# Where the inverse is applied in a chunked delta rule: to the decayed keys ahead of the scan, or to beta v minus keys times state inside it

## The chip, the cores and the metric

The kernel runs on one core of one Trainium2 chip. The metric is the device time of one execution in microseconds (us), the median of several runs. The engines are named as in the profile: PE is the matrix engine (PEld its weight loads), DVE the vector engine, ACT the scalar engine, POOL the engine that here makes small sums and DMA issues, SP the queue that issues the weight loads.

## The reference

Two transformer-like blocks on 512 tokens of width 1024. The first block has a gated delta-rule layer (8 heads, keys of 128, values of 256) and a windowed attention layer; the second has four feed-forward layers, a pooling layer and a convolution module. The change is in the delta rule alone:

```python
def step(S, inp):                      # one chunk; every head has a state S of (128, 256)
    qk_i, qd_i, kd_i, u_i, w_i, gl_i = inp
    v_new = u_i - w_i @ S
    o = qd_i @ S + qk_i @ v_new
    S = S * gl_i + kd_i.T @ v_new
    return S, o
# ahead of the loop, for each chunk:
#   decay = exp(g[:, None] - g[None, :]) below the diagonal, g a running sum of log decays
#   lower = strict_lower(beta * (k @ k.T) * decay)
#   u, w  = solve(I + lower, [beta * v, beta * exp(g) * k])
#   qk = (q @ k.T) * decay;  qd = q * exp(g);  kd = k * exp(g_last - g);  gl = exp(g_last)
```

The kernel takes chunks of 128 tokens, so there are 4 chunks where the reference has 8 of 64; the result is the same sum.

## The kernel before, in words

**Order of stages.** Each engine has its own list of instructions, written out by hand, and semaphores tie them together. The delta-rule layer comes first and ends at about 557 us. It works through 4 pairs of heads (`pe_a`, `act_a`, `dve_a`, `gp_a`, called with i = 0 to 3). The `Marks` objects `a_pe`, `a_act`, `a_dve` and `a_gp` count the named steps of each engine, and `wait` waits for a step by its name.

**Filler.** The weights come in tiles of 128x2048. ACT rounds a tile (L354), DVE subtracts the rounded part from the raw one (`split_tile`, L359), and PE multiplies with both parts, three matmuls for one product. While PE works on a pair of heads it also makes the projections for the gate of this pair and for the queries, keys and values of the next one: six tiles of 16 steps, 96 steps in all, each of three matmuls (L768 to L770). `pe_filler` hands them out: `fill(n)` issues the next n steps, and `fill()` all that are left. A pair before the last one spends its 96 steps as 55 ahead of the scan over the chunks (up to the `fill(2)` of L897), 16 in the scan (two behind the `vn` products of each chunk and two behind the `sn` products), 6 behind the scan (L929), and the last 19 behind the column sums `os` (L939). The last pair has only 32 steps, since there is no next pair, and they run out with chunk 0 of the scan. Behind the filler of a pair stand its two output tiles (L941, which calls `pe_tile`: 16 chunks of 6 matmuls, L382 to L384).

**The scan.** For each chunk c and each of the two heads a, PE makes `vn`: `inv_T` times `v_beta` (L909) and, from chunk 1 on, `neg_wT` times `state` into the same accumulator (L911). ACT copies it to `v_new` (L1052). PE makes the outputs `o` (L921, L922) and the update of the state `sn` (L926). DVE writes the new `state` (L1239 in chunk 0, L1242 after it). `neg_wT` is made ahead of the scan: DVE multiplies the turned keys with beta and decay (`k_bg`, L1179), PE multiplies that with `inv_T` (`nw`, L901), and ACT copies it with the sign turned (L1046). In float32 each product is two instructions of the trace.

**DVE beside the scan.** Its list is: `convolved(0)` (two L1114, six L1117) for the next pair, the two states of chunk 0, `split(4)`, the states of chunks 1 and 2, `convolved(2)`, `split(5)`, the four gated outputs `og` (L1253), and, once the norm of the output is there, `gt` (L1261), `split(6)`, the pair of rounded outputs (L1093), `convolved(4)`, and only then `add_chunks` (L427), which adds the output tile to `xT` chunk by chunk. A chunk n of the output tiles may start on PE only when DVE has added chunk n - 4 (the wait on `out_free` in `pe_tile`), since there are four PSUM banks for them. The norm itself runs from `os` on PE over two logarithms (L1067) and two exponentials (L1070) on ACT, then `take(5)` (L955), a rounding (L354) and the rounded outputs (L1076).

## Time and profile before

| | |
|---|---|
| median of 3 runs | 2715.42 us (2711.14 to 2717.76) |
| the profiled execution | 2712.42 us |
| its span, first to last instruction | 2710.8 us |
| mean granted PE clock | 0.983 |
| busy share PE, PEld, DVE, ACT, POOL | 97%, 78%, 57%, 37%, 13% |
| DMA | 238 MB, mean 88 GB/s |

A time in the trace counts from the start of the span. Busy shares are over the whole span; a matmul's busy time includes its way through the array, so the distance from start to start of successive matmuls is what one costs in a row of them. The first pair of heads occupies PE from about 87 to 213 us, the second to 340 us, the third to 467 us, and the last one to about 557 us.

### The profile page before, as it was taken

The page shows a single profiled execution, that of the slowest core. Times are in us where ns is not written, and L with a number is a line of the kernel's source. Part 1 is how long each engine was busy: PE and PEld are TensorE (multiplying, and loading weights), DVE is VectorE, ACT ScalarE, POOL GpSimd, SP SyncE. Part 2 cuts the span into 40 slices and gives each one's busy share as a digit, 9 for nine tenths or more (in the row PEclk, how much of TensorE's full clock was granted, in tenths as well). Part 3 has the DMA queues.
Part 4 walks back from the last instruction along what each step waited for, and adds up shares of the span by engine and source line. Part 5 has one row for each costly group of instructions (what it writes and reads, how often), then busy time and mean ns, then how long its engine had stood idle before and what let it go on. Part 6 is the DMA issues. An engine that isn't in the chain of part 4 may idle for free.

```text
span 2710.8 us, 37439 instructions
## 1 busy us (share of the span) xinstructions
PE 2631.8 (97%) x14593; PEld 2112.3 (78%) x14593; DVE 1547.4 (57%) x2261; ACT 1001.1 (37%) x1414; POOL 360.9 (13%) x330
## 2 busy tenths in 40 slices
PE   7999999899999979999999999999999897999998
PEld 5787878687777758888888888888888664888887
DVE  6666756576666664454555444654444776644445
ACT  4544444446556542222252222332222313422223
POOL 1110101022000011111131111121112120211110
PEclk8999999999999979999989999999999998999999
DMA  3222223122222212222312322222322452222321
GB/s 114 82 84 72 78 64 98 43 71 78 78 85 77 75 50 94 93 93 96 105 47 93 102 99 93 93 94 98 103 93 94 119 157 56 94 93 94 106 94 62
DMA packets 171509, 238.23 MB, mean 88 GB/s; under 512 B 6513, under 2 KB 149371, under 8 KB 171411
## 3 DMA queue, kind: packets, MB, share of 16 engines
q1 hardware_dynamic: 163523, 217.23, 24.2%
q0 software_dynamic: 6080, 19.43, 2.6%
q8 instruction: 69, 1.13, 0.2%
q10 hardware_dynamic: 1808, 0.21, 0.1%
q14 instruction: 29, 0.24, 0.0%
HBM read 232.36 MB, written 4.40 MB: 87 GB/s over the span
## 4 chain that ended last, share of the span: by engine, by line
PE 88%; DVE 5%; DMA 2%; ACT 2%; issue 2%; POOL 1%; DVEq 0%; SPq 0%; ACTq 0%; POOLq 0%
PE ps L382 20%; PE ps L383 20%; PE ps L384 20%; PE ps L768 5%; PE ps L770 4%; PE ps L769 4%; PE ps L368 1%; DVE w_lo L359 1%; PE ps L370 1%; PE ps L369 1%; DMA glu_scratch<-glu 1%; DVE probs L1633 1%; PE ps L1491 1%; PE ps L1502 1%; DMA shifted<-glu_scratch 1%
## 5 line engine op out<-in xcount | busy, mean ns | idle before, releaser
L354 ACT ACTIVATE w_hi<-w_raw 128x2048 fp32r<-128x2048 f32 x203 | 388.5, 1914 | 911.6 <-PE ps L384 901.5
L382 PE MATMUL ps<-h_hi,w_hi 128*128 128x512 f32 x1456 | 567.7, 390 | 0.0
L384 PE MATMUL ps<-h_hi,w_lo 128*128 128x512 f32 x1456 | 566.6, 389 | 0.0
L383 PE MATMUL ps<-h_lo,w_hi 128*128 128x512 f32 x1456 | 566.4, 389 | 0.0
L359 DVE TENSOR_TENSOR w_lo<-w_raw,w_hi 128x2048 fp32r<-128x2048 f32 x203 | 464.8, 2290 | 129.5 <-ACT w_hi L354 129.4
L427 DVE SCALAR_TENSOR_TENSOR xT<-ps,xT 128x512 f32<-128x512 f32 x504 | 336.5, 688 | 146.8 <-PE ps L384 145.7
L382 PE MATMUL ps<-a_hi,w_hi 128*128 128x512 f32 x1024 | 401.8, 392 | 17.1 <-issue 17.1
L383 PE MATMUL ps<-a_lo,w_hi 128*128 128x512 f32 x1024 | 401.1, 392 | 0.0
L384 PE MATMUL ps<-a_hi,w_lo 128*128 128x512 f32 x1024 | 400.9, 392 | 0.0
L1718 POOL TENSOR_TENSOR f_gate<-f_gate,n_rstd 128x512 f32<-128x512 f32 x88 | 176.9, 2012 | 1121.8 <-ACT f_gate L1712 1121.8
L382 PEld LDWEIGHTS ps<-h_hi,w_hi 128*128 128x128 f32 x1456 | 273.3, 188 | 59.3 <-issue 2.5
L384 PEld LDWEIGHTS ps<-h_hi,w_lo 128*128 128x128 f32 x1456 | 273.3, 188 | 56.7
L383 PEld LDWEIGHTS ps<-h_lo,w_hi 128*128 128x128 f32 x1456 | 273.3, 188 | 56.6
L768 PE MATMUL ps<-h_hi,w_hi 128*128 128x512 f32 x608 | 260.2, 428 | 1.4 <-DVE w_lo L359 1.4
L382 PEld LDWEIGHTS ps<-a_hi,w_hi 128*128 128x128 f32 x1024 | 194.1, 190 | 60.1 <-issue 19.5
L770 PE MATMUL ps<-h_hi,w_lo 128*128 128x512 f32 x608 | 238.1, 392 | 0.0
L769 PE MATMUL ps<-h_lo,w_hi 128*128 128x512 f32 x608 | 237.3, 390 | 0.0
L383 PEld LDWEIGHTS ps<-a_lo,w_hi 128*128 128x128 f32 x1024 | 194.0, 190 | 40.4
L384 PEld LDWEIGHTS ps<-a_hi,w_lo 128*128 128x128 f32 x1024 | 193.8, 189 | 40.5
L1772 DVE TENSOR_TENSOR f_hid<-f_gate,ps 128x512 f32<-128x512 f32 x88 | 60.5, 688 | 252.6 <-PE ps L384 246.3
L1763 DVE TENSOR_TENSOR f_gate<-ps,n_rstd 128x512 f32<-128x512 f32 x88 | 60.5, 691 | 233.2 <-PE ps L384 233.1
L768 PEld LDWEIGHTS ps<-h_hi,w_hi 128*128 128x128 f32 x608 | 114.1, 188 | 40.2 <-issue 16.1
(337 smaller groups left out, 2820.9 us busy)
## 6 DMA issues: line engine op xcount, KB each, us to landing
w_raw<-in_ffn_w_in_dram SPq DMA_DIRECT2D x88, 1024.0 KB, 5.0
w_raw<-in_ffn_w_out_dram SPq DMA_DIRECT2D x44, 1024.0 KB, 4.8
w_raw<-in_a_w_in_dram SPq DMA_DIRECT2D x24, 1024.0 KB, 5.3
w_raw<-in_b_w_in_dram SPq DMA_DIRECT2D x16, 1024.0 KB, 5.4
w_raw<-in_conv_w_pw_dram SPq DMA_DIRECT2D x12, 1024.0 KB, 5.7
shifted<-glu_scratch POOLq DMA_DIRECT2D x32, 264.0 KB, 4.7
w_raw<-in_a_w_out_dram SPq DMA_DIRECT2D x8, 1024.0 KB, 4.8
w_raw<-in_b_w_out_dram SPq DMA_DIRECT2D x8, 1024.0 KB, 4.8
```

The costliest lines, as they stand in the source:

```text
L354: nc.scalar.activation(w_hi[:, t % 2], w_raw[:, t % 2], ACT.Copy).then_inc(hi_done, 1)
L359: nc.vector.tensor_tensor(w_lo[:, t % 2], w_raw[:, t % 2], w_hi[:, t % 2].bitcast(F32), ALU.subtract).then_inc(lo_done, 1)
L382: nc.tensor.matmul(dst, wh, xh, start=(k == 0), stop=False)
L383: nc.tensor.matmul(dst, wh, xl, start=False, stop=False)
L384: m = nc.tensor.matmul(dst, wl, xh, start=False, stop=last)
L427: ins = nc.vector.scalar_tensor_tensor(xT[:, n], src, scale, xT[:, n], ALU.mult, ALU.add)
L768: nc.tensor.matmul(dst, wh[:, w], h_hi[:, k], start=k == 0, stop=False)
L769: nc.tensor.matmul(dst, wh[:, w], h_lo[:, k], start=False, stop=False)
L770: ins = nc.tensor.matmul(dst, wl[:, w], h_hi[:, k], start=False, stop=k == KC - 1)
L1718: nc.gpsimd.tensor_tensor(f_gate[:, c], f_gate[:, c], n_rstd[:], ALU.mult).then_inc(f_gated, 1)
L1763: nc.vector.tensor_tensor(f_gate[:, c], ps[:, c], n_rstd[:], ALU.mult).then_inc(in_free, 1)
L1772: nc.vector.tensor_tensor(f_hid[:, c], f_gate[:, c], ps[:, 2 + c], ALU.mult).then_inc(in_free, 1)
```

## The change

The product of the inverse with the decayed keys is no longer made. Instead, in chunks 1 to 3, PE multiplies the keys with the state (`ks`), DVE scales the result with beta and decay and subtracts `v_beta` from it (`r`, written over `v_beta`), and PE multiplies the inverse with that (`vn`). The sign is turned in ACT's copy. `k_bg`, `nw` and `neg_wT` are gone. In the scan a `fill(2)` (`fill(1)` in the last pair) stands between `ks` and `vn`; DVE's two `r` of a chunk stand behind its two states, ahead of `split(4)` in chunk 0.

```diff
--- before.py
+++ after.py
@@ -232,7 +232,7 @@
             z_gate = sb("z_gate", [P, 4, T], into=s)
         rel_in, rel_T = z_gate[0:BUCKETS, 2, 0:B_HEADS], z_gate[0:B_HEADS, 2, P:P + BUCKETS]
         rel_line = z_gate[0:B_HEADS, 3, 0:3 * P]
-        inv_T, neg_wT, k_bg = g_wide, decay, expg
+        inv_T = g_wide
 
 
         binv_T, binv = b_wide[:, 0, 0:8 * BK], b_wide[:, 0, 8 * BK:16 * BK]
@@ -609,23 +609,23 @@
                      + [x for l in lv for x in [f"A{l}", f"X{l}"]
                         + ([f"vt{a}{l - 2}" for a in heads] if l in (2, 3) else [])]
                      + ["A5", "X5", "A6", "X6"]
-                     + [f"nw{a}" for a in heads]
-                     + [f"{x}{c}{a}" for c in range(TC) for x in (("vn", "o", "sn") if c < TC - 1 else ("vn", "o"))
+                     + [f"{x}{c}{a}" for c in range(TC)
+                        for x in [y for y in ("ks", "vn", "o", "sn") if not (y == "ks" and c == 0 or y == "sn" and c == TC - 1)]
                         for a in heads]
                      + [f"os{a}" for a in heads])
         a_act = Marks(sem("a_act"), [f"sq{c}" for c in (2, 3, 0, 1)] + [f"ln{c}" for c in (2, 3, 0, 1)]
                       + [f"rs{c}" for c in (2, 3, 0, 1)]
                       + [f"eg{a}" for a in heads] + [f"d{a}" for a in heads]
                       + ["blocks", "dg"]
-                      + [f"nw{a}" for a in heads] + [f"vn{c}{a}" for c in range(TC) for a in heads]
+                      + [f"vn{c}{a}" for c in range(TC) for a in heads]
                       + [f"os{a}{d}" for a in heads for d in range(2)] + [f"oln{a}" for a in heads]
                       + [f"ors{a}" for a in heads])
         a_dve = Marks(sem("a_dve"), [f"nrm{c}" for c in (2, 3, 0, 1)]
                       + [f"{x}{a}" for a in heads for x in ("db", "lt")] + ["u0", "u1", "T0", "qk0", "qd0"]
-                      + ["P1", "qk1", "qd1", "U1", "T1", "kb0", "kd0", "P2", "kb1", "kd1", "U2", "T2"]
+                      + ["P1", "qk1", "qd1", "U1", "T1", "kd0", "P2", "kd1", "U2", "T2"]
                       + ["P3", "vb00", "vb01", "U3", "T3", "P4", "vb10", "vb11", "U4", "T4"]
                       + ["P5", "U5", "P6", "U6"]
-                      + [f"S{c}{a}" for c in range(TC - 1) for a in heads]
+                      + [f"{x}{c}{a}" for c in range(TC - 1) for x in ("S", "r") for a in heads]
                       + [f"og{a}{d}" for a in heads for d in range(2)]
                       + [f"gt{a}{d}" for a in heads for d in range(2)])
         a_gp = Marks(sem("a_gp"), [f"msk{a}" for a in heads] + ["zero"] + [f"osum{a}" for a in heads])
@@ -895,26 +895,20 @@
                          inv_T[hi, a, c * P + 64:c * P + P], start=True, stop=True)
             a_pe.done("X6", ins)
             fill(2)
-            for a in heads:
-                a_dve.wait(pe, "U6", i)
-                for c in range(TC):
-                    ins = mm(pb(2 + a, c), v(k_bg, a, c), v(inv_T, a, c), start=True, stop=True)
-                a_pe.done(f"nw{a}", ins)
+            a_dve.wait(pe, "U6", i)
             for c in range(TC):
+                if c:
+                    for a in heads:
+                        a_dve.wait(pe, f"S{c - 1}{a}", i)
+                        a_pe.done(f"ks{c}{a}", mm(ps[:, 4 + a, 0:A_DV], v(qkv, 2 + a, c), state[:, a], start=True, stop=True))
+                    fill(2 if ahead > 1 else 1)
                 for a in heads:
-                    b = ps[:, 4 + a, 0:A_DV]
                     if c:
-                        a_dve.wait(pe, f"S{c - 1}{a}", i)
-                        a_act.wait(pe, f"nw{a}", i)
-                    ins = mm(b, v(inv_T, a, c), v_beta[:, a, c], start=True, stop=c == 0)
-                    if c:
-                        ins = mm(b, v(neg_wT, a, c), state[:, a], start=False, stop=True)
-                    a_pe.done(f"vn{c}{a}", ins)
-                fill(1 if last_pair(i) else 2)
+                        a_dve.wait(pe, f"r{c - 1}{a}", i)
+                    a_pe.done(f"vn{c}{a}", mm(ps[:, 4 + a, 0:A_DV], v(inv_T, a, c), v_beta[:, a, c], start=True, stop=True))
+                fill(2 if ahead > 1 else 1)
                 for a in heads:
                     a_act.wait(pe, f"vn{c}{a}", i)
-                    if c == 0:
-                        a_act.wait(pe, "nw1", i)
                     for d in range(2):
                         b = pb((2, 3, 6, 7)[2 * a + d], c)
                         if c:
@@ -1041,15 +1035,12 @@
             a_act.done("dg", ins)
             take(1)
             rounded(4)
-            for a in heads:
-                a_pe.wait(act, f"nw{a}", i)
-                a_act.done(f"nw{a}", fn(neg_wT[:, a], ps[:, 2 + a], ACT.Copy, scale=-1.0))
             for c in range(TC):
                 for a in heads:
                     a_pe.wait(act, f"vn{c}{a}", i)
                     if c:
                         a_pe.wait(act, f"sn{c - 1}{a}", i)
-                    a_act.done(f"vn{c}{a}", fn(v_new[:, a], ps[:, 4 + a, 0:A_DV], ACT.Copy))
+                    a_act.done(f"vn{c}{a}", fn(v_new[:, a], ps[:, 4 + a, 0:A_DV], ACT.Copy, scale=-1.0 if c else 1.0))
                 if c == 0:
                     take(2)
                 elif c == 2:
@@ -1176,7 +1167,6 @@
                 wide = lambda name, n: gate_col(name, i, a).to_broadcast([P, TC, n])
                 a_pe.wait(dve, f"kt{a}", i)
                 a_dve.wait(dve, f"qd{a}", i)
-                a_dve.done(f"kb{a}", v.tensor_tensor(by_chunk(k_bg[:, a]), by_chunk(ps[:, 2 + a]), wide("beta_exp", P), ALU.mult))
                 a_dve.done(f"kd{a}", v.tensor_tensor(by_chunk(k_dec[:, a]), by_chunk(ps[:, 2 + a]), wide("k_decay", P), ALU.mult))
 
             def values(d):
@@ -1241,6 +1231,11 @@
                         decayed = gate["last"][:, c, bass.ds(i * 2 + a, 1)]
                         ins = v.scalar_tensor_tensor(state[:, a], state[:, a], decayed, ps[:, 4 + a, A_DV:], ALU.mult, ALU.add)
                     a_dve.done(f"S{c}{a}", ins)
+                for a in heads:
+                    a_pe.wait(dve, f"ks{c + 1}{a}", i)
+                    a_dve.done(f"r{c}{a}", v.scalar_tensor_tensor(
+                        v_beta[:, a, c + 1], ps[:, 4 + a, 0:A_DV], gate["beta_exp"][:, c + 1, bass.ds(i * 2 + a, 1)],
+                        v_beta[:, a, c + 1], ALU.mult, ALU.subtract))
                 if c == 0:
                     split(4)
             convolved(2)
```

## Rows read from the trace of the kernel before

**Rows 1.** The page: engines' busy time, the chain that ended last, a weight load.
```profile
PE 2631.8 (97%) x14593; PEld 2112.3 (78%) x14593; DVE 1547.4 (57%) x2261; ACT 1001.1 (37%) x1414; POOL 360.9 (13%) x330
...
PE 88%; DVE 5%; DMA 2%; ACT 2%; issue 2%; POOL 1%; DVEq 0%; SPq 0%; ACTq 0%; POOLq 0%
...
w_raw<-in_a_w_in_dram SPq DMA_DIRECT2D x24, 1024.0 KB, 5.3
```

**Rows 2.** PE's waits, 80 to 560 us: total us, times, longest.
```profile
PE ps L382 <- issue: 6.5, 1, 6.5
PE ps L768 <- DVE w_lo L359: 1.4, 1, 1.4
PE ps L851 <- DVE b_wide L1199: 0.3, 1, 0.3
```

**Rows 3.** Timeline of PE, first pair, chunks 0 to 2: start us, us, instruction, count.
```profile
145.09 1.95 PE L901 MATMUL ps<-g_wide,expg 128*128 128x128 f32 x16
146.88 1.03 PE L909 MATMUL ps<-v_beta,g_wide 128*128 128x256 f32 x4
...
152.28 0.59 PE L909 MATMUL ps<-v_beta,g_wide 128*128 128x256 f32 x2
152.71 0.59 PE L911 MATMUL ps<-state,decay 128*128 128x256 f32 x2
...
159.44 0.59 PE L909 MATMUL ps<-v_beta,g_wide 128*128 128x256 f32 x2
```

**Rows 4.** Timeline of DVE and ACT, same stretch; in brackets idle before, and releaser.
```profile
145.09 4.05 DVE L1117 SCALAR_TENSOR_TENSOR qkv<-conv_in,cols,qkv 128x512 f32<-128x512 f32 x6
...
151.43 2.28 DVE L359 TENSOR_TENSOR w_lo<-w_raw,w_hi 128x2048 fp32r<-128x2048 f32 x1
...
165.80 0.88 DVE L1114 TENSOR_SCALAR qkv<-conv_in,cols 128x512 f32<-128x512 f32 x2
...
170.57 2.29 DVE L359 TENSOR_TENSOR w_lo<-w_raw,w_hi 128x2048 fp32r<-128x2048 f32 x1
...
153.34 0.38 ACT L1052 ACTIVATE v_new<-ps 128x256 f32<-128x256 f32 x1 [4.11 <-PE ps L911]
```

**Rows 5.** DVE's groups by shape, 80 to 560 us: count, busy us, mean ns.
```profile
L1242 DVE SCALAR_TENSOR_TENSOR state<-state,gate_last,ps 128x256 f32<-128x256 f32 x16 | 7.3, 480 | 39.1 <-PE ps L926 39.1
...
L1179 DVE TENSOR_TENSOR expg<-ps,gate_beta_exp 128x512 f32<-128x512 f32 x8 | 5.3, 666 | 0.0
```

**Rows 6.** Timeline of PE behind the scan, first pair.
```profile
176.97 1.88 PE L937 MATMUL ps<-square,ones 128*128 128x512 f32 x4
178.29 0.79 PE L768 MATMUL ps<-h_hi,w_hi 128*128 128x512 f32 x1
...
179.39 0.40 PE L768 MATMUL ps<-h_hi,w_hi 128*128 128x512 f32 x1
...
190.98 0.39 PE L768 MATMUL ps<-h_hi,w_hi 128*128 128x512 f32 x1
191.66 0.39 PE L382 MATMUL ps<-a_hi,w_hi 128*128 128x512 f32 x1
...
197.10 0.39 PE L382 MATMUL ps<-a_hi,w_hi 128*128 128x512 f32 x1
...
213.42 0.39 PE L768 MATMUL ps<-h_hi,w_hi 128*128 128x512 f32 x1
```

**Rows 7.** Timelines of ACT and DVE behind the scan, first pair.
```profile
181.95 0.58 ACT L955 ACTIVATE conv_in<-ps 128x512 f32<-128x512 f32 x1
...
189.78 4.06 DVE L1117 SCALAR_TENSOR_TENSOR qkv<-conv_in,cols,qkv 128x512 f32<-128x512 f32 x6
193.75 1.52 DVE L427 SCALAR_TENSOR_TENSOR xT<-ps,xT 128x512 f32<-128x512 f32 x2
195.94 0.69 DVE L427 SCALAR_TENSOR_TENSOR xT<-ps,xT 128x512 f32<-128x512 f32 x1 [0.67 <-PE ps L384]
197.30 0.69 DVE L427 SCALAR_TENSOR_TENSOR xT<-ps,xT 128x512 f32<-128x512 f32 x1 [0.67 <-PE ps L384]
...
211.86 2.48 DVE L427 SCALAR_TENSOR_TENSOR xT<-ps,xT 128x512 f32<-128x512 f32 x4
```

**Rows 8.** Timeline of the last pair's scan.
```profile
515.17 0.86 DVE L1239 COPY state<-ps 128x256 f32<-128x256 f32 x2 [5.57 <-PE ps L926]
...
516.09 0.59 PE L909 MATMUL ps<-v_beta,g_wide 128*128 128x256 f32 x2
...
520.78 0.70 PE L909 MATMUL ps<-v_beta,g_wide 128*128 128x256 f32 x2
...
521.31 0.59 PE L911 MATMUL ps<-state,decay 128*128 128x256 f32 x2
...
522.61 0.38 PE L921 MATMUL ps<-qn,state 128*128 128x128 f32 x2
...
528.96 0.39 PE L922 MATMUL ps<-qk_T,v_new 128*128 128x128 f32 x2
```

**Rows 9.** Windows: length; busy us of PE, PEld, DVE, ACT, POOL; granted clock; DMA.
```profile
521.00:526.00 5.00, 4.86 (x30) 4.17 (x30) 1.12 (x4) 3.17 (x4) 0.00 (x0) 1.00 0.00 0
...
534.00:540.00 6.00, 0.17 (x1) 0.20 (x2) 3.98 (x7) 4.92 (x8) 0.00 (x0) 0.78 0.00 0
540.00:544.00 4.00, 4.00 (x10) 3.13 (x11) 1.62 (x3) 0.00 (x0) 0.00 (x0) 0.50 0.02 4
```

## The prediction

> **What bounds the kernel now.** I read the page first. PE is busy 97% of the span and carries 88% of the chain that ended last [rows 1]. Then I listed PE's waits in the stretch of the delta rule. In some 470 us it waits 6.5 us once (ahead of the last pair's output tiles), 1.4 us once, and a few tenths besides [rows 2]. So the three pairs with full filler, from 87 to 467 us, are PE back to back, and there only two things count: PE work that goes, and a wait that appears. The last pair has no filler in chunks 1 to 3 and shows its own chain. Last I read the timelines of the scan and of what follows it, to see how far the other engines run ahead of PE. The reader should look at the places where PE and DVE nearly meet. In the first pair DVE adds the first chunk of the output tile at 193.75 to 194.44 (0.69 us, the duration of one L427) [rows 7], and PE, which may not start chunk 4 before that, starts it at 197.10 [rows 6]. The slack is 2.66 us. The three pairs repeat each other to 0.1 us.
>
> **What the change removes.** The `nw` products are 16 instructions of PE, from 145.09 to the next product at 146.88: 1.79 us a pair [rows 3], 7.2 us in four pairs. Two DVE operations of 0.67 us [rows 5] and two ACT copies a pair go as well. DVE and ACT wait for PE around there, in the full pairs and nearly so in the last, so I count these at nothing. The Trainium skill, page "TensorE: Matmul & The Clock Gate", section "Back-to-back issue gap", has about 81 ns for each matmul of 128 columns in a stream of loads and matmuls. By it the 64 instructions would be an estimated 5.2 us. The row has 1.79 / 16 = 0.112 us, and the sum goes by the row.
>
> **What it adds on PE: nothing in number.** From chunk 1 on `ks` takes the place of the `neg_wT` product and `vn` that of the `inv_T` product, both 128x256 in two instructions of 0.22 us (0.43 us from 152.28 to 152.71) [rows 3].
>
> **The new wait inside the scan, full pairs.** PE now needs DVE's `r` between `ks` and `vn`. A result of PE is read 0.63 us after its product starts (L911 at 152.71, the copy at 153.34) [rows 3, 4]. `r` is not in the trace; the nearest row is L1242, same form and size, one operand in PSUM: 0.48 us [rows 5]. Bounds are 0.4 and 0.7 us. So `r` of the first head ends 1.1 us behind the start of `ks`, that of the second 1.6 us. PE comes to `vn` after two `ks` (0.87 us) and two filler steps (1.36 us), at 2.2 us, and to the second head's at 2.7. The slack is 1.1 us for both, more than the upper bound takes. Cost nothing; without this cover 0.4 to 0.7 us in each of nine chunks.
>
> **What queues behind `r` on DVE.** In chunk 0 it is `split(4)`, which was made from 151.43 [rows 4]. It moves to about 152.1 to 154.4; its tile is wanted from step 65, about 158.3. In chunk 2 it is `convolved(2)` and `split(5)`. A chunk took 7.16 us (152.28 to 159.44) [rows 3] and takes 8.5 with two more filler steps. `convolved(2)`, from 165.80 before, waits for `r` of chunk 3 and starts at about 169.1, and `split(5)` ends at about 176.2 where it ended at 172.9 [rows 4]. Its tile is wanted at step 81, now at about 177.3. The slack of 1.1 us is thin, but it holds. SP's load of the tile two further on starts after each split and takes 5.3 us [rows 1]; `split(5)` releases that of the second output tile, whose rounding comes some 16 us later.
>
> **The filler that moves.** This is the part that costs. Three more blocks of two steps are spent in the scan of a full pair, and the total of 96 doesn't grow. So 13 steps instead of 19 are left behind `os`. Between 176.97 and 191.66 PE covered the norm, the gating and the rounding of the outputs [rows 6], which start with `os` and keep their length. A step is 0.68 us (18 from 179.39 to 191.66) [rows 6], so PE comes 6 x 0.68 = 4.1 us sooner to the output tile, counted from `os`. First it meets `take(5)` on ACT, which frees the bank for step 89: done 5.6 us behind `os` (182.53 - 176.97) [rows 7], wanted five steps behind `os`, at 2.42 + 4 x 0.68 = 5.1 (2.42 from 176.97 to 179.39, `os` and one step) [rows 6], a stall of 0.4. Then it meets the first `add_chunks`, behind `convolved(4)` in DVE's list, which ends 17.47 us behind `os` (194.44 - 176.97). PE wants chunk 4 at 20.13 - 4.08 = 16.05 us. The stall is 1.42 us in all, the first one included. From there DVE has no idle time to give back: its list up to the last addition fills 19.2 us (193.75 to 214.34 without the two idle times of 0.67) [rows 7], and PE's 12 chunks of 1.36 and the next pair's first 4 steps, behind which the additions must be done, fill 19.1. So each full pair gains 1.79 - 1.42 = 0.37 us, three gain 1.1. Bounds: 0 (DVE needs a further 0.4 us there) and 1.79 a pair (no stall).
>
> **The last pair.** It gains the 1.79 us of `nw`. Its filler ends in chunk 0 before and after, so `r` lies bare in chunks 1 to 3. Before, PE restarted 0.04 us behind `state` (520.78), and `o` followed 1.83 us behind that (522.61) [rows 8]. Now, counted from `ks`: `r` of the first head may start at 0.10 + 0.63 (a restart costs 0.10, as 520.78 to 521.31 is 0.53 where 0.43 is usual) and ends at 1.2. `vn` runs from 1.25, its result can be read at 1.25 + 0.10 + 0.63 = 2.0, and ACT's copy of 0.38 us [rows 4] ends at 2.4. `o` starts at about 2.45 or, with another restart, as at 2.5: 0.65 us later than before, in three chunks 1.95 us. Bounds by `r` of 0.4 and 0.7 us: 1.7 and 2.6. The pair nets +0.2 (-0.1 to +0.8).
>
> **The sum.** -3 x 0.37 + 0.2 = -0.9 us. The profiled execution took 2712.4 us (span 2710.8), so 2711.5 on its own scale. The median of the three runs is 3.0 us above it; the same change from there gives 2714.5 us. That is 0.03%. What a measurement of this kernel can tell from no change is about 0.3%, 8.1 us.
>
> **Rivals.**
> - *The whole of `nw` is won.* DVE's tail isn't met, since the filler steps or DVE's list run otherwise than I add them up. Full pairs give -5.4, the last +0.2: 2710.2 us; with the last pair's `r` free too, 2708.3. For it: PE is the bound by the page. Against it: the slack of 2.66 us is smaller than the 4.1 us that move. Chance 0.12. It too stays within 0.3%.
> - *DVE's list breaks the cover further.* `r` or `split(5)` comes late, or chunks 10 to 15 of the outputs wait for DVE. With 1 us more in each full pair it is 2717.5 us, with 2 us 2720.5. Against it are the slacks above. Chance 0.14.
> - *The other side: PE's clock falls in the last pair's scan.* In 534 to 540 us PE is busy 0.17 of 6 us, the granted clock there averages 0.78, and it is 0.50 in the next 4 us, the lower of its two levels, 1.2 GHz [rows 9]. In 521 to 526, with PE busy 4.86 of 5 us, it stayed at 1.00. The change adds two or three short waits a chunk to the 0.5 us there. If that made it fall, the 13 us from 516.09 to 528.96 [rows 8] would nearly double: +12 us, 2726 us, slower by 0.4%. It decides if the granted clock of these windows is below about 0.7 throughout. The page named above, section "HAM oscillation", warns of just this, a half clock from idle time between bursts of matmuls; whether such short gaps do it no row here shows. Chance 0.04.
> - *The change is not neutral before the scan.* Something that I count as covered, such as the missing `k_bg` on DVE in the last pair's short filler, speeds up its chain by the 2.7 us of four operations at most: 2711.8 us. Chance 0.05.
>
> **Numbers.** My forecast has 0.65, and the cases above follow. Likeliest 2714.5 us. The range goes from 2708.3 (all won) to 2720.5 (2 us more of DVE in each pair), 2708 to 2721; outside it lie the clock's case and a part of what the medians scatter. Faster by over 0.3% (below 2707.3) would need more than the 7.2 us that go away: 0.03. Slower (above 2723.6) is the clock's case and a rest of the second: 0.06. Within: 0.91.
>
> **What would show it.** In the trace after, `nw` is gone and DVE's `r` is an operation of 0.48 us, 24 times (three chunks, two heads, four pairs); PE waits for it only in the last pair, about 0.3 us each time. In each full pair PE waits about 0.4 us at a filler step (for ACT, L955) and 1 us at chunk 4 of the first output tile (for DVE, `add_chunks`). The distance from pair to pair is 126.6 us instead of 126.9. A pair distance of 125.1 shows the first rival right, one of 127 or more the second. The granted clock of the last scan shows the third.

## The result and the profile after

In nine runs of each kernel on one chip, the kernel before had a median of 2717.76 us (2711.14 to 2719.65) and the changed kernel 2723.78 us (2714.09 to 2731.73). The ratio on record is 1.0028, with an interval of 1.0015 to 1.0040; it is not the quotient of the two medians, which is 1.0022. By the medians the change is slower by 6.0 us, a little under what I had said such a measurement can tell; with nine runs the interval leaves 1 out. The profiled execution took 2730.16 us, with a span of 2727.6 us against 2710.8 before. The forecast was 2714.5 us, 2708 to 2721, so the result lies outside its range.

The page of the changed kernel, its first line of busy time and its chain, the counterpart of [rows 1]:

```profile
PE 2641.4 (97%) x14529; PEld 2114.4 (78%) x14529; DVE 1551.7 (57%) x2277; ACT 996.8 (37%) x1406; POOL 361.1 (13%) x330
...
PE 86%; DVE 6%; ACT 2%; DMA 2%; issue 2%; POOL 1%; DVEq 0%; ACTq 0%; POOLq 0%
```

PE has 64 instructions fewer, the `nw` products, and yet its busy time is 9.6 us longer. Part of this work must have been done at a lower clock: the mean granted clock is 0.978 where it was 0.983. The waits of PE from 80 to 575 us (in total, times, longest) say where to look; beside them, [rows 2] has three:

```profile
PE ps L382 <- issue: 6.5, 1, 6.5
PE ps L382 <- DVE xT L427: 2.2, 3, 0.7
PE ps L858 <- issue: 2.0, 1, 2.0
PE ps L768 <- DVE w_lo L359: 1.4, 1, 1.4
PE ps L768 <- ACT conv_in L949: 0.8, 3, 0.3
```

Two of the new lines come three times, once in each pair with full filler, and are the stalls of the forecast. The third comes once and was in no part of the forecast: 2.0 us at L858, the small products of the inverse (step `X4`), and nothing that the profile shows released PE from it. It lies in the last pair. PE's timeline there:

```profile
498.61 0.39 PE L770 MATMUL ps<-h_hi,w_lo 128*128 128x512 f32 x1
498.93 0.43 PE L858 MATMUL ps<-b_wide 32*32 32x32 f32 x26
501.41 0.63 PE L858 MATMUL ps<-b_wide 32*32 32x32 f32 x38 [2.05 <-issue]
501.97 0.80 PE L768 MATMUL ps<-h_hi,w_hi 128*128 128x512 f32 x1
```

The 64 products of one burst are cut after the 26th. No wait stands in the program between them, and in the kernel before they took 0.75 us in one piece. What follows the hole is the greater loss. Windows of the changed kernel (columns as in [rows 9]; the last three are granted clock, DMA share, GB/s):

```profile
497.00:498.00 1.00, 1.00 (x66) 0.64 (x64) 0.00 (x0) 0.00 (x0) 0.00 (x0) 1.00 1.09 387
498.00:499.00 1.00, 1.00 (x22) 0.56 (x14) 0.85 (x2) 0.00 (x0) 0.00 (x0) 1.00 0.90 313
499.00:500.00 1.00, 0.36 (x26) 0.25 (x26) 0.77 (x2) 0.00 (x0) 0.00 (x0) 1.00 0.03 9
500.00:501.00 1.00, 0.00 (x0) 0.00 (x0) 0.00 (x0) 0.00 (x0) 0.00 (x0) 1.00 0.05 6
501.00:502.00 1.00, 0.59 (x39) 0.53 (x39) 0.00 (x0) 0.00 (x0) 0.00 (x0) 0.81 0.00 0
502.00:504.00 2.00, 2.00 (x23) 1.25 (x21) 0.87 (x2) 0.34 (x1) 0.00 (x0) 0.50 0.03 8
...
516.00:518.00 2.00, 2.00 (x6) 1.60 (x5) 0.14 (x1) 0.00 (x0) 0.00 (x0) 0.50 0.00 0
518.00:520.00 2.00, 2.00 (x9) 1.61 (x8) 0.00 (x0) 0.77 (x2) 0.00 (x0) 0.83 0.00 0
```

The same windows of the kernel before:

```profile
498.00:499.00 1.00, 1.00 (x66) 0.64 (x64) 0.00 (x0) 0.00 (x0) 0.00 (x0) 1.00 1.08 383
499.00:500.00 1.00, 1.00 (x22) 0.58 (x17) 0.87 (x2) 0.00 (x0) 0.00 (x0) 1.00 0.86 301
500.00:501.00 1.00, 1.00 (x66) 0.91 (x67) 1.00 (x3) 0.00 (x0) 0.00 (x0) 1.00 0.09 28
```

PE does nothing in 500 to 501, and from 502 to 518 the granted clock is 0.50, the lower level of 1.2 GHz, though PE is busy all the time. Before, it stayed at 1.00. The hole and the half clock together are the loss of the last pair: from the start of the last pair (L816, at 468.96 after and 469.99 before) to its first output tile it is 79.34 us where it was 69.84. The tile in the timelines, first after, then before:

```profile
548.30 0.76 PE L382 MATMUL ps<-a_hi,w_hi 128*128 128x512 f32 x1 [6.50 <-issue]
```

```profile
539.83 0.77 PE L382 MATMUL ps<-a_hi,w_hi 128*128 128x512 f32 x1 [6.50 <-issue]
```

That is 9.5 us more. Of the 16.8 us by which the two profiled spans differ, most of the rest are 4.9 us in the pooling stage, which has a second stretch at half clock at 1399 to 1413 us, and 3.5 us in the convolution stage. Both come back to below.

**What arrived late.** In both kernels the 1 MB load of `w_kv`, the weights of the attention stage, comes over the DMA engines at this time: in the windows above it fills them up to 499 after, and up to 500 before. The trace also has the transfers that bring PE's instructions, in blocks of 16 KB on a queue of their own (q8, 68 blocks in the run). From 493 us on the changed kernel has no such block until 499.0. The kernel before has one at 495.3, just ahead of the load's first packets (496.5). In straight parts of the program one block comes for every 256 or so instructions of PE: from the one at 482.0 to the one at 531.7 us it is 1545 instructions for six blocks. While PE goes round a loop, as from 713 to 926 us, none comes.

By 499.0 PE had started 438 instructions since the block before; elsewhere in the last pair it was 116 to 302, and before 176 to 353. The change takes 40 PE instructions out of each pair (160 in all, 30233 to 30073, those that the profile doesn't count as busy included), so the borders of the blocks fall at other places of the program.

### The profile page after: what moved, and what is told of

It is laid out like the page before. It is cut to its first block, busy times and chain, and to the rows that moved or that the text cites. A ratio compares the mean times of both kernels' runs of the same rounds, so it can differ in the third digit from the quotient of the medians.

```text
span 2727.6 us, 37287 instructions
## 1 busy us (share of the span) xinstructions
PE 2641.4 (97%) x14529; PEld 2114.4 (78%) x14529; DVE 1551.7 (57%) x2277; ACT 996.8 (37%) x1406; POOL 361.1 (13%) x330
## 3 DMA queue, kind: packets, MB, share of 16 engines
q8 instruction: 68, 1.11, 0.2%
## 4 chain that ended last, share of the span: by engine, by line
PE 86%; DVE 6%; ACT 2%; DMA 2%; issue 2%; POOL 1%; DVEq 0%; ACTq 0%; POOLq 0%
PE ps L382 20%; PE ps L384 20%; PE ps L383 20%; PE ps L768 4%; PE ps L770 4%; PE ps L769 4%; DVE w_lo L359 1%; DMA glu_scratch<-glu 1%; PE ps L368 1%; PE ps L370 1%; PE ps L369 1%; DVE probs L1628 1%; PE ps L1486 1%; PE ps L1497 1%; DMA shifted<-glu_scratch 1%
## 5 line engine op out<-in xcount | busy, mean ns | idle before, releaser
L382 PE MATMUL ps<-a_hi,w_hi 128*128 128x512 f32 x1024 | 402.3, 393 | 19.2 <-issue 17.1
L427 DVE SCALAR_TENSOR_TENSOR xT<-ps,xT 128x512 f32<-128x512 f32 x504 | 335.5, 687 | 142.1 <-PE ps L384 141.6
```

What stands on the lines that cost most here:

```text
L382: nc.tensor.matmul(dst, wh, xh, start=(k == 0), stop=False)
L427: ins = nc.vector.scalar_tensor_tensor(xT[:, n], src, scale, xT[:, n], ALU.mult, ALU.add)
```

## The experiments

**Theory S (supply).** PE ran out of instructions: the block that it needed at `X4` of the last pair was fetched late, because the load of `w_kv` held the DMA engines. The hole then let the clock fall. The change causes it only through the place of a block's border. **Rival T (tail).** The loss is the change's own: DVE's list and the bare `r`, as in the rivals of the forecast. **Rival N (noise).** The half clock comes and goes by itself and the first nine runs fell unluckily.

The texts below that were written ahead of the runs call S theory F. Their theory C is a part of T: the bare waits of the last scan lower the clock.

Medians in us; ratio to the kernel before, measured beside it on the same chip (its medians were 2717.8 for the first nine runs, 2717.0 beside after_again, the pads of 136 and 120 and after_late_load, 2718.3 beside after_again2, before_gap2 and after_balanced, and 2717.2 beside the rest), with its interval; stage: from the end of PE's first long wait behind 80 us, where the work for the first pair begins, to the last pair's first output tile, in the one profiled execution.

| run | median (range), runs | ratio [interval] | stage |
|---|---|---|---|
| before, first profile | 2717.8 (2711.1 to 2719.7), 9 | 1 | 453.5 |
| after, first profile | 2723.8 (2714.1 to 2731.7), 9 | 1.0028 [1.0015, 1.0040] | 462.8 |
| after_again | 2721.3 (2717.5 to 2732.2), 12 | 1.0021 [1.0009, 1.0033] | 454.5 |
| after_again2 | 2724.8 (2716.4 to 2728.8), 12 | 1.0022 [1.0012, 1.0031] | 457.9 |
| after_late_load | 2719.2 (2711.1 to 2725.8), 12 | 1.0003 [0.9991, 1.0016] | 453.0 |
| before_late_load | 2716.6 (2711.4 to 2719.7), 11 | 0.9998 [0.9989, 1.0007] | 452.9 |
| before_pad136 | 2733.2 (2726.3 to 2735.5), 5 | 1.0063 [1.0050, 1.0076] | 454.2 |
| after_pad120 | 2723.4 (2716.6 to 2734.2), 8 | 1.0035 [1.0021, 1.0050] | 453.5 |
| after_pad60 | 2722.2 (2713.8 to 2726.0), 11 | 1.0013 [1.0001, 1.0025] | 461.9 |
| before_load_x4 | 2715.3 (2710.2 to 2718.1), 11 | 0.9991 [0.9982, 1.0000] | 453.0 |
| before_gap2 | 2725.6 (2724.4 to 2728.7), 6 | 1.0031 [1.0019, 1.0042] | 459.3 |
| after_balanced | 2715.7 (2712.2 to 2723.2), 12 | 0.9993 [0.9983, 1.0003] | 454.2 |
| after_balanced_late | 2713.8 (2707.5 to 2720.0), 12 | 0.9985 [0.9974, 0.9995] | 448.1 |

**The changed kernel, run again.** No edit.

> The changed kernel itself, once more. In its first profile PE stood still for 2.05 us in the middle of a burst of small products (L858) at 499 us, where it waited for nothing that the profile shows, and from 502 us its clock was at the lower level for 17 us. Theory F (late instruction fetch): that stall is bound to a place in PE's instruction stream. A block of 16 KB of instructions was fetched at 499.0 us, 438 PE instructions after the one before it where some 250 are usual, and a weight load was under way just then. It then comes again at the same place in the stream, with 1 to 2.5 us, and the spread of the times (2714 to 2732) comes from whether the clock falls behind it. Theory C (bare waits of the last scan lower the clock): no stall at L858 is needed and the clock falls in chunks 1 to 3 of the last pair. Both expect a median of 2718 to 2730.

> The changed kernel for a third profile. Theory F: a stall of 1 to 2.5 us at L858 again, at the same place in the stream. With the clock falling the stretch from the end of PE's first long wait to the last pair's output tile is 461 to 463 us, without it 454 to 455 us. Median 2719 to 2724 us.

The loss is there in each of three sets of runs, with 1 outside each interval, so rival N falls as to the whole. In both of these profiles the burst `X4` is cut at the same place as in the first. This is after_again:

```profile
498.49 0.43 PE L858 MATMUL ps<-b_wide 32*32 32x32 f32 x26
500.08 0.54 PE L858 MATMUL ps<-b_wide 32*32 32x32 f32 x38 [1.16 <-issue]
```

The hole is in all three profiles of the unedited changed kernel; its size differs. With 1.16 us idle the clock held, and the last pair took 71.01 us (468.77 to 539.78), 1.4 us more than without a hole (69.65, below). In after_again2 it was 2.04 us, and 6.8 us at half clock followed; its stage of 457.9 us lies between the two values that I had expected.

**The load moved away.** SP issues the load only once PE has done `X6` of the last pair, some 12 us later (its first packets come at 508.1 instead of 495.7). The same edit in the kernel before is the control.

```diff
+            a_pe.wait(sp, "X6", A_PAIRS - 1)
             for k in range(2):
                 load(sp, T_KV + k, cols256(w_kv, ...
```

> The changed kernel with the load of the first key-value weight tile (1 MB, on SP's queue, at 494.5 us) held until the last pair's X6 products (about 509 us); it is wanted at about 550 us. PE's instruction stream is the same. Theory F, with the weight load as what makes the fetch late: the fetch comes some 250 instructions after the one before, at about 496 us, no stall, no half clock from 502 us, and 2709 to 2718 us. If the border in the stream alone makes the stall and the load has no part in it, the stall stays and so does the time, 2718 to 2730 us.

> Control for the late load: the kernel before with that load held until X6 (about 509 us). In the kernel before no fetch of PE collided with it to any harm, so both theories expect the same time as before, 2711 to 2719 us. If this is faster by 2 us or more, the late load helps by itself and the gain of the changed kernel with the late load says nothing of the fetch.

In the changed kernel the burst is whole again (first line), the clock stays at 1.00, and the DMA share shows the load gone from this window (0.03 where it was 0.90 to 1.09):

```profile
498.42 0.75 PE L858 MATMUL ps<-b_wide 32*32 32x32 f32 x64
```

```profile
495.00:500.00 5.00, 5.00 (x157) 3.55 (x145) 3.60 (x8) 0.00 (x0) 0.00 (x0) 1.00 0.03 7
500.00:505.00 5.00, 4.89 (x107) 3.72 (x106) 1.79 (x5) 2.97 (x7) 0.00 (x0) 1.00 0.01 3
```

The block of instructions that was fetched at 499.0 (497.6 in after_again) now comes at 495.6, 277 instructions behind the last. The stages of the two kernels are 453.0 and 452.9 us: without the collision the change neither wins nor loses there. The ratios are 1.0003 and 0.9998, no difference from the kernel before in either. This is the main evidence against rival T, since `r` and the moved filler are all still there. The median is weaker evidence than the rows: 2719.2 us is above the 2709 to 2718 that I had expected, and within the rival's range. The profiled execution of after_late_load even took 2725.6 us, with a stage of 453.0. Its excess lies elsewhere: the pooling stage took 756.7 us (751.7 in the control) and the convolution stage 599.5 (592.6), with more of both at half clock.

**The block's border moved.** Idle instructions on PE ahead of the first product shift every later border in the program. Up to `X4` of the last pair the change takes out 120 instructions (three pairs of 40). 120 pads in the changed kernel give the old borders back, 136 in the kernel before shift them on by as much as makes 256 with the missing 120, and 60 in the changed kernel go half the way.

```diff
             pe.sem_inc(chunk_done, CHUNK_CREDIT)
+            for _ in range(136):            # 120, 60 in the changed kernel
+                pe.sem_inc(pad_sem, 1)
             pe.wait_ge(setup_const, FIRST_CONSTS)
```

> The kernel before, with 136 instructions that only count up an unused semaphore put on PE's list ahead of its first work, where PE waits some 10 us for the input in any case. No other line differs. The change took 40 PE instructions out of each pair, so 120 ahead of the last pair's bursts; with blocks of 256 instructions, 136 more put the block borders where the change has them. Theory F: PE stalls 1 to 2 us within the bursts of the last pair, the clock falls behind it, and the time is 2716 to 2730 us, slower than before by 0.1 to 0.5%. Theory C and the theory that the change's own work costs the time: same as before, 2711 to 2720 us, with no stall.

> The changed kernel with 120 such instructions ahead of PE's first work, so that the block borders lie in the last pair's bursts where they lay before the change. Theory F: no stall above 0.3 us at L858 and no half clock from 502 to 519 us; 2709 to 2717 us, 5 to 9 us under the changed kernel. Theory C: no effect, 2718 to 2730 us, and the clock falls in the last scan.

> The changed kernel with 60 instructions that only count up an unused semaphore ahead of PE's first work. One takes 0.15 us on PE (20.5 us for 136 in an earlier run), so 60 take 9.1 us and lie within the 10.6 us that PE waits for the input: the shift costs no time here, while 136 and 120 of them had put off the start by 10.9 and 8.7 us. The block border then falls about 60 PE instructions earlier in the last pair's bursts, and the fetch is asked for at about 495.2 us, ahead of the packets of the weight load (495.9 to 499). Theory F: no stall at L858, no half clock from 502 us, median 2714 to 2719 us against about 2722 for the changed kernel. A theory in which the change's work itself costs the time: 2720 to 2724 us.

The kernel before, with 136 pads and nothing of the change in it, shows the cut at the same product:

```profile
510.74 0.43 PE L859 MATMUL ps<-b_wide 32*32 32x32 f32 x26
512.00 0.54 PE L859 MATMUL ps<-b_wide 32*32 32x32 f32 x38 [0.82 <-issue]
```

With 120 pads the changed kernel has no hole, no half clock in this stretch, and a stage of 453.5 us. The median, 2723.4 us, missed the 2709 to 2717 that I had expected, and so did the 2733.2 of before_pad136, expected at 2716 to 2730. The pads were not free as I had meant them to be. One takes 0.15 us, so 136 fill 20.8 us and 120 fill 18.4, and the wait for the input that should cover them lasts only 10.5 us. The work for the first pair begins at 97.2 us instead of 86.3 with 136 and at 94.1 instead of 85.5 with 120. Less these 10.8 and 8.6 us the medians are 2722.3 and 2714.7, against 2717.0 of the kernel before beside them. So the padded kernel before comes out near the time of the changed one, and the padded changed kernel somewhat below before. The correction comes from one profile each, and without pads this start lies anywhere from 84.9 to 86.3 us, so it is weaker than the rows. The profile of before_pad136 is of the fastest of its five runs (2726.3 us). It shows the hole but no half clock behind it, in a stage 1.2 us over that of before_late_load; that the clock fell in the slower runs isn't shown.

With 60 pads, which the wait for the input does cover, I had expected no hole and 2714 to 2719 us. The median was 2722.2; there was a hole, of 1.47 us, and 17.1 us at half clock behind it. But it had moved:

```profile
496.55 0.74 PE L852 MATMUL ps<-b_wide,lower_T 32*32 32x32 f32 x63
498.76 0.21 PE L852 MATMUL ps<-b_wide,lower_T 32*32 32x32 f32 x1 [1.47 <-issue]
```

It now cuts the burst before, `A4`, ahead of its last product. From there to the 26th product of `X4` stand 1 + 3 + 26 = 30 matmuls, each with its weight load, so 60 instructions: just the number of pads. Counted in PE's instructions, the hole stands behind number 8897 in all four unpadded runs of the changed kernel that have it and again with 60 pads, and behind number 9153 in before_pad136, 256 further on. It sits at a fixed place of the stream of instructions, one of a row 256 apart (a block of 16 KB is then 64 bytes an instruction), and not at an operation of the kernel. For theory S this miss says more than a hit would have. It was the expectation that was careless. It had the load's packets begin at 495.9 us, and they began at 494.7; PE passed the border ahead at 494.15, and a fetch starts 0.9 to 1.4 us behind that even when nothing holds it (next experiment), so it met the load again.

**A late block made on purpose.** In the kernel before, the load waits for `X4` instead of `X6`, so that it falls on the next block.

```diff
+            a_pe.wait(sp, "X4", A_PAIRS - 1)
```

> The kernel before, PE's stream untouched, but the load of the first key-value weight tile is held until the X4 products (about 500.7 us), so that its packets lie at about 501 to 505 us, where a block of PE's instructions was fetched at 503.6 us. Theory F: that fetch comes late, at about 505 us, and PE stalls 0.5 to 2 us in the bursts behind it; where the clock falls after that the time grows by some 8 us: median 2718 to 2726 us, 2 to 8 us over the kernel before. If a fetch isn't held up by a weight load, or nothing is lost by it: 2711 to 2719 us and no stall.

The load filled the DMA engines as planned, and the block came at 504.1, 324 instructions behind the last. PE never stopped:

```profile
502.00:503.00 1.00, 1.00 (x36) 0.88 (x26) 0.59 (x2) 0.98 (x3) 0.00 (x0) 1.00 1.06 369
503.00:504.00 1.00, 1.00 (x6) 0.55 (x6) 0.66 (x2) 0.08 (x1) 0.00 (x0) 1.00 0.59 207
```

The expectation missed, in time and in rows: a late block alone isn't enough. In the runs with a hole the block came after 438, 434, 449, 419 and 406 instructions, but with 60 pads after 301, so the count since the last block doesn't tell. What does is how far PE still is from the border. With the borders at 8385, 8641, 8897, 9153 and 9409 of PE's instructions (256 apart, as the holes have them), the traces give the time at which PE passes each. At 8641 the next block's fetch starts 0.9 to 1.4 us behind that in the eight profiles in which no load was in the way. The fetches that met the load came up to 3.8 us behind, the latest ones as the load drained:

| run | fetch starts | behind the last border | instructions to the next | PE reaches it | PE goes on | from fetch to going on |
|---|---|---|---|---|---|---|
| after | 498.99 | 3.8 | 36 | 499.17 | 501.41 | 2.42 |
| after_again | 497.62 | 2.8 | 56 | 498.74 | 500.08 | 2.46 |
| after_again2 | 499.12 | 3.7 | 41 | 499.32 | 501.55 | 2.43 |
| after_balanced | 494.38 | 3.8 | 25 | 494.52 | 496.76 | 2.38 |
| after_pad60 | 496.42 | 2.3 | 126 | 497.09 | 498.76 | 2.34 |
| before_pad136 | 509.64 | 2.6 | 75 | 510.99 | 512.00 | 2.36 |
| before | 500.04 | 1.4 | 154 | 502.09 | 502.44 | 2.40 |
| after_pad120 | 507.58 | 1.3 | 188 | 509.82 | 509.87 | 2.29, no hole |
| before_gap2 | 498.89 | 1.3 | 188 | 503.91 | 503.92 | 5.03, no hole |
| before_load_x4 | 504.10 | 3.6 | 121 | 511.49 | 511.49 | 7.39, no hole |

In each of the seven holes PE goes on 2.3 to 2.5 us behind the start of the fetch. So in these rows a fetch costs nothing when PE has about that much work left ahead of the border, and otherwise what is missing. In before_load_x4 the block was as late as in the changed kernel, but the 121 instructions left, among them waits and 128x512 products, lasted 7.4 us. The table also shows that the kernel before already had such a hole, of 0.15 us, at the border 9153:

```profile
501.66 0.62 PE L868 MATMUL ps<-b_wide,lower_T 32*32 32x32 f32 x27
502.44 0.28 PE L868 MATMUL ps<-b_wide,lower_T 32*32 32x32 f32 x5 [0.15 <-issue]
```

The full list of its waits, of which [rows 2] shows three, has a line for it:

```profile
PE ps L868 <- issue: 0.2, 1, 0.2
```

**The hole by itself.** In the kernel before, 14 idle instructions in the same burst of the last pair, after its 24th product, with the load and, up to there, the blocks as they were.

```diff
                 for k, a, c in combos:
+                    if k == 3 and l == 4 and last_pair(i):
+                        for _ in range(14):
+                            pe.sem_inc(pad_sem, 1)
                     for r in ROWS:
```

> The kernel before with 14 instructions that only count up an unused semaphore put in the middle of the last pair's X4 burst (L858), where the changed kernel has its stall: at 0.15 us each PE's matrix part stands still for about 2.1 us. Nothing else differs. Two ways to read the changed kernel: (1) the stall costs its own length and sometimes the clock. Then PE's way from the end of its first long wait to the last pair's output tile is about 455 us where the clock holds and about 462 us where it falls, and the median lies 3 to 8 us above the kernel before: 2720 to 2725 us. (2) The stall is harmless and the half clock has another cause in the changed kernel: only 2 us more, 2717 to 2720 us, and the clock never falls at 500 us.

PE was idle for 1.80 us, and the clock fell at once:

```profile
500.00:505.00 5.00, 3.86 (x77) 2.92 (x78) 1.29 (x3) 1.45 (x4) 0.00 (x0) 0.57 0.03 10
505.00:510.00 5.00, 5.00 (x58) 3.25 (x57) 1.25 (x3) 1.51 (x4) 0.00 (x0) 0.50 0.00 0
510.00:515.00 5.00, 5.00 (x43) 4.19 (x44) 1.38 (x2) 0.00 (x0) 0.00 (x0) 0.91 0.00 0
```

The stage is 459.3 us, 5.8 more than in the first profile of before: the hole itself and some 4 us lost over the 10 us at half clock. The median rose by 7.3 us (from the 2718.3 of before). So a hole of 1.8 us here is enough for a loss as large as the changed kernel's, with nothing else of the change. The Trainium skill, page "TensorE: Matmul & The Clock Gate", section "HAM oscillation", has idle time between bursts of matmuls as what brings the half clock; these rows agree in kind.

**The filler spread otherwise.** The forecast's stalls behind the scan come from six filler steps that moved into it. Here `fill(1)` stands after `ks`, and two steps after `vn` in chunk 0 alone, so that the scan takes about as many as before.

```diff
-                    fill(2 if ahead > 1 else 1)              # after ks
+                    fill(1)
...
-                fill(2 if ahead > 1 else 1)                  # after vn
+                fill(2 if ahead > 1 and c == 0 else 1)
```

> The changed kernel with the filler put back (19 steps behind os) and the weight load left where it was. It is the version with the late load less the late load, so it tells what each gives. Theory F: the last pair's fetch meets the weight load again, PE stalls 1 to 2 us at L858 and the clock falls in some executions; median 2716 to 2721 us, 3 to 7 us over the version with both (2713.8). If the late load does nothing: 2712 to 2716 us and no stall.

> The changed kernel with the late load and with the filler of a full pair put back: in chunks 1 to 3 one step behind ks, one behind vn and two behind sn, so that 19 steps are again left behind os instead of 13. The forecast had it that the 6 steps moved cost 1.4 us of stall in each full pair, in front of DVE's first addition. If so, those stalls (0.3 us for ACT, 0.7 us for DVE in the profile after) are gone, r and the copies stay covered (1.1 us each against 1.5 us of PE work), each full pair gains 1.0 to 1.5 us on the changed kernel, and the median is 3 to 4.5 us under that of the changed kernel with the late load alone (2719): 2714 to 2716 us. If r or the copies are no longer covered, PE shows waits in chunks 1 to 3 and the gain is smaller or gone.

PE's waits for L427 and L949 are gone from both. In after_balanced_late, which has the later load too, the first and the last pair start at

```profile
88.58 3.59 PE L816 MATMUL ps<-square,ones 128*128 128x512 f32 x8
463.94 3.59 PE L816 MATMUL ps<-square,ones 128*128 128x512 f32 x8
```

which is (463.94 - 88.58) / 3 = 125.12 us a pair, against 126.93 before: 1.81 us, the whole of `nw`. The cut of the burst is still there in after_balanced (2.04 us idle, 10.2 us at half clock, stage 454.2) and gone with the later load (448.1). The medians show less of this than the rows: I had expected after_balanced at 2716 to 2721 us, and it came at 2715.7, only 1.8 us above the version with the later load. At 2713.8 us that version beats both kernels, by 0.15% of the one before (ratio 0.9985, 0.9974 to 0.9995).

## Why the prediction was wrong

**The step that failed** is in the sum: that the last pair is touched only by `nw` (-1.79) and the bare `r` (+1.95), and so nets +0.2. The last pair took 9.5 us more. I priced what the change does to the work on each engine and to the semaphores. Its effect on the stream of instructions itself, 160 fewer on PE, had no term. That effect brought the fetch of a block under the load of `w_kv` with a burst of small products ahead of the border. It cost 1.4 to 9.7 us in the last pair, as the hole was short or the clock fell behind it. Nor is the whole of the number's miss the change's: of the 9.3 us between forecast and median, 2.3 lie in the kernel before, whose median of three runs, from which I had started, was 2715.4 and of nine 2717.8. My rival on the stretch before the scan had it the other way, 2.7 us faster. The rival on the other side named the half clock, but at the wrong place and by the wrong cause; that its kind of loss appeared is luck.

**The full pairs: mechanism right, size off.** Forecast was 0.37 us gained in each. The pairs start at 88.36, 215.20, 342.10 and 468.96, so 126.87 us a pair; before it was 126.93. The gain is 0.06 us. PE's timeline behind the scan of the first pair, against [rows 6]:

```profile
178.51 1.88 PE L931 MATMUL ps<-square,ones 128*128 128x512 f32 x4
...
183.45 0.39 PE L770 MATMUL ps<-h_hi,w_lo 128*128 128x512 f32 x1
184.12 0.50 PE L768 MATMUL ps<-h_hi,w_hi 128*128 128x512 f32 x1 [0.28 <-ACT conv_in L949]
184.45 0.40 PE L769 MATMUL ps<-h_lo,w_hi 128*128 128x512 f32 x1
...
194.92 0.39 PE L384 MATMUL ps<-a_hi,w_lo 128*128 128x512 f32 x1
196.03 0.50 PE L382 MATMUL ps<-a_hi,w_hi 128*128 128x512 f32 x1 [0.72 <-DVE xT L427]
```

Both stalls are where they were forecast, at a filler step for ACT and at chunk 4 of the output tile for the additions. The reader should measure them by starts and not by the idle time in brackets. From 183.45 to 184.12 it is 0.67 us where 0.23 is usual, and the next start is 0.33 on instead of 0.23: 0.54 us. At 196.03 it is 1.11 instead of 0.23, 0.88, and a restart of about 0.1 again. That is 1.5 us; the brackets show 1.0. From `os` to the next pair it is 36.69 us, where the old 39.17 less six steps of 0.68 would be 35.09: a loss of 1.60 where I had 1.42. The term left out was the restart, 0.1 us behind each of the two waits, which I did count in the last pair. The other 0.1 us was lost ahead of `os`, which came 90.15 us behind its pair's start instead of 87.76 (2.39 later, forecast 2.29).

**`r` in the scan: right.** It took 484 ns (forecast 0.48), and PE has no wait for it in a full pair. DVE stood idle before it (timeline of DVE, first pair):

```profile
150.27 0.92 DVE L1236 SCALAR_TENSOR_TENSOR v_beta<-ps,gate_beta_exp,v_beta 128x256 f32<-128x256 f32 x2 [1.32 <-PE ps L903]
151.10 2.28 DVE L359 TENSOR_TENSOR w_lo<-w_raw,w_hi 128x2048 fp32r<-128x2048 f32 x1
...
168.99 4.06 DVE L1108 SCALAR_TENSOR_TENSOR qkv<-conv_in,cols,qkv 128x512 f32<-128x512 f32 x6
172.96 2.29 DVE L359 TENSOR_TENSOR w_lo<-w_raw,w_hi 128x2048 fp32r<-128x2048 f32 x1
```

`split(4)` and `split(5)` each end a microsecond sooner than I had them (153.4 and 175.3, forecast 154.4 and 176.2), and PE's list of waits has no new one for a split.

**The last pair's scan: right.** The `ks` of chunks 1 to 3 and their `vn` (timeline of PE, against [rows 8]), and windows over the scan:

```profile
522.41 1.03 PE L903 MATMUL ps<-state,qkv 128*128 128x256 f32 x4
523.58 1.13 PE L908 MATMUL ps<-v_beta,g_wide 128*128 128x256 f32 x4
...
527.81 1.13 PE L903 MATMUL ps<-state,qkv 128*128 128x256 f32 x4
...
533.32 1.13 PE L903 MATMUL ps<-state,qkv 128*128 128x256 f32 x4
```

```profile
521.00:526.00 5.00, 4.81 (x27) 3.58 (x26) 1.76 (x4) 0.77 (x2) 0.00 (x0) 1.00 0.00 2
526.00:532.00 6.00, 5.68 (x35) 4.15 (x34) 1.83 (x4) 2.11 (x4) 0.00 (x0) 1.00 0.01 3
```

Chunks follow each other at 5.40 and 5.51 us, before at 4.69 (516.09 to 520.78, [rows 8]) and 4.78: 0.7 us each for the bare `r`, forecast 0.65. From the first `ks` to the first `vn` it is 1.17 us where four such instructions take 0.87: 0.3 for `r`, as forecast. With the later load in both kernels the whole last pair takes 69.66 us after and 69.43 before, so +0.23, as forecast. The clock stayed at 1.00 in chunks 1 to 3 of this scan in every profile. The rival of short gaps between `ks` and `vn` is refuted for this kernel.

**The other rivals.** That all of `nw` is won didn't come with this filler, but it is what after_balanced_late does. That DVE breaks the cover further came true by 0.3 us a pair.

**What stays open.** Two parts of the first profile's 16.8 us: a second stretch at half clock in the pooling stage and 3.5 us in the convolution stage. With the second stretch the pooling stage takes 756.6 to 759.5 us, without it 751.7. It is there in four of the eight profiles of the changed kernel and its variants (after, after_again, after_late_load, after_balanced_late) and in two of the five of the kernel before (before_load_x4, before_gap2). The convolution stage, from its first wait to the end, varies from 589.3 to 592.8 us among the profiles of the kernel before and from 587.1 to 599.5 among the others. Both kernels have both, and whether the change makes them more frequent isn't settled. For the medians this matters: the profiles put 1.4 to 9.7 us on the hole, the medians of the changed kernel are 4 to 6 us up, and taking the hole away by the later load brings back the ratio from 1.0021 to 1.0003, with intervals that still overlap, and in the balanced version by less than 0.001. The rows show the hole's cause and price in the stage; how much of the median's rise is the hole isn't settled.

## What to carry to other kernels

Where PE is busy throughout, look in its waits for a burst cut by "issue", compare the time of the instruction queue's blocks with that of the big loads, and move the load before judging the change. Even a short cut of this kind, as the 0.15 us here, tells that PE came to the end of a block ahead of the next one. A hole of 2 us on a busy PE cost two to five times its length here through the clock, so a load placed without a thought can outweigh an edit worth 1.8 us a pair. When work goes from one part of a hand-filled schedule, fill steps have to be spread again: here that made the difference between 0.06 and 1.81 us a pair.

## What the runs showed of the hardware that was not expected

- PE's instructions come over the same DMA engines as the weights, in blocks of 16 KB (68 on q8, 1.11 MB). Under a 1 MB load at a DMA share of 0.9 to 1.1 one came late and PE stood still for 0.8 to 2.05 us (0.15 in the kernel before), in the middle of a burst of 32x32 products. PE went on 2.3 to 2.5 us behind the start of the fetch, in seven profiles. A block just as late (3.6 us behind the last border) cost nothing where PE had 7.4 us of work ahead of the next one.
- The granted clock fell to 0.50 after holes of 1.47, 1.80, 2.04 and 2.05 us and held after those of 0.82 and 1.16. It stayed down for 6.8 to 17.1 us, with PE busy throughout; in the stage this and the hole cost 4.9 (6.8 us at half clock) to 9.7 us (17.1). The length of a hole alone doesn't decide it: behind the same wait of 2.03 us in the convolution stage the clock stayed at 1.00 in the kernel before (L2002, 2249 us) and fell to 0.50 in after_again2 (L1997, 2252 us).
- A semaphore increment on PE took 0.15 us, start to start, in a row of 136 ahead of the first product as well as in the 14 in the burst, which made a hole of 1.8 us.
